# SSD slots of a two-block transformer kernel: ScalarE's queue re-ordered, C B formed ahead of the transposes and read ahead of the convolution

## The reference

```python
def ssd_mixer(h, w_in, conv_w, conv_b, dt_bias, a_log, d_skip, norm_g, w_out):
    z, xbc, dt = split(h @ w_in)
    xbc = silu(causal_depthwise_conv(xbc, conv_w, conv_b))      # 4 taps
    xs, b_in, c_in = split(xbc)
    dt = softplus(dt + dt_bias); a = -exp(a_log)
    a_cs = cumsum(dt * a)                                       # along the tokens
    decay = exp(where(causal, a_cs[l] - a_cs[s], -inf))
    cb = einsum('bclgn,bcsgn->bcgls', c_c, b_c)
    y = einsum('bcgjls,bcsgjp->bclgjp', cb * decay, x * dt) + ...
    y = y + xs * d_skip
    g = y * silu(z)
    g = g * rsqrt(mean(g * g, per group) + EPS) * norm_g
    return g @ w_out
```

## Time and profile before

| | us |
|---|---|
| median of 3 runs | 1209.87 (1209.8 to 1210.95) |
| profiled execution, its own time | 1210.28 |
| its span in the trace | 1208.6 |
| PE busy | 1148.3 (95%) |
| DVE busy | 754.4 (62%) |
| ACT busy | 674.9 (56%) |
| POOL busy | 186.3 (15%) |

### The profile page before, as it was taken

How to read it: one execution, slowest core, us unless ns; L and a number is a source line. 1 busy time by engine, 2 the same in 40 slices (tenths; PEclk the granted TensorE clock), 3 DMA queues, 4 the chain that set the end, 5 groups by cost and what they waited for, 6 DMA issues and landing times.

```text
span 1208.6 us, 23743 instructions
## 1 busy us (share of the span) xinstructions
PE 1148.3 (95%) x8898; PEld 1089.9 (90%) x8898; DVE 754.4 (62%) x1123; ACT 674.9 (56%) x1071; POOL 186.3 (15%) x134
## 2 busy tenths in 40 slices
PE   6999999999999999679988999999999999999998
PEld 5988988899999999556657999999998999999998
DVE  4788778768665554536646666555678678666543
ACT  4788888755554343457735555444554665555332
POOL 0443444317000001022301000000000212000000
PEclk8999999999999999779979999999999999999999
DMA  5554344395555554222203555565544555555553
GB/s 192 179 173 151 130 158 154 113 256 159 180 174 168 182 165 157 88 86 88 80 26 111 186 191 181 183 192 179 170 159 125 172 185 184 188 177 188 192 179 99
DMA packets 53225, 190.32 MB, mean 157 GB/s; under 512 B 5920, under 2 KB 7072, under 8 KB 53168
## 3 DMA queue, kind: packets, MB, share of 16 engines
q1 hardware_dynamic: 51408, 182.95, 47.0%
q0 software_dynamic: 1760, 6.59, 1.8%
HBM read 188.44 MB, written 1.08 MB: 157 GB/s over the span
## 4 chain that ended last, share of the span: by engine, by line
PE 75%; DVE 8%; issue 8%; ACT 5%; POOL 3%; DMA 1%; ACTq 0%; DVEq 0%; POOLq 0%; SPq 0%
PE lin L412 23%; PE lin L414 22%; PE lin L413 22%; DVE w_lo L1207 2%; POOL w_lo L1747 1%; ACT w_hi L826 1%; POOL y L1765 1%; PE lin L641 1%; PE ps L682 1%; PE ps L683 1%; PE lin L639 1%; DVE cv L1286 1%; PE ps L445 1%; DVE rot_a L1509 0%; DVE x_lo L1217 0%
## 5 line engine op out<-in xcount | busy, mean ns | idle before, releaser
L1207 DVE TENSOR_TENSOR w_lo<-w_raw,w_hi 128x1024 fp32r<-128x1024 f32 x303 | 381.3, 1260 | 273.1 <-ACT w_hi L826 273.0
L826 ACT ACTIVATE w_hi<-w_raw 128x1024 fp32r<-128x1024 f32 (+2 forms) x343 | 354.3, 1040 | 244.3 <-PE lin L414 239.9
L412 PE MATMUL lin<-x_hi,w_hi 128*128 128x256 f32 (+1 forms) x1528 | 445.4, 291 | 11.0 <-DVE x_lo L1233 3.7
L414 PE MATMUL lin<-x_hi,w_lo 128*128 128x256 f32 (+1 forms) x1528 | 439.0, 287 | 0.0
L413 PE MATMUL lin<-x_lo,w_hi 128*128 128x256 f32 (+1 forms) x1528 | 438.2, 287 | 0.0
L412 PEld LDWEIGHTS lin<-x_hi,w_hi 128*128 128x128 f32 x1528 | 292.0, 191 | 15.2 <-DVE x_lo L1233 4.1
L413 PEld LDWEIGHTS lin<-x_lo,w_hi 128*128 128x128 f32 x1528 | 291.5, 191 | 1.4 <-issue 1.0
L414 PEld LDWEIGHTS lin<-x_hi,w_lo 128*128 128x128 f32 x1528 | 292.3, 191 | 0.0
L414 PE MATMUL lin<-hid_hi,w_lo 128*128 128x256 f32 (+1 forms) x768 | 218.2, 284 | 0.0
L413 PE MATMUL lin<-hid_lo,w_hi 128*128 128x256 f32 (+1 forms) x768 | 217.9, 284 | 0.0
L412 PE MATMUL lin<-hid_hi,w_hi 128*128 128x256 f32 (+1 forms) x768 | 217.4, 283 | 0.0
(11 more groups left out here) (252 smaller groups left out, 1515.7 us busy)
## 6 DMA issues: line engine op xcount, KB each, us to landing
w_raw<-w SPq DMA_DIRECT2D x343, 512.0 KB, 3.3
acs_bc<-acs_dram POOLq DMA_DIRECT2D x8, 544.0 KB, 4.9
bias_mask<-rpb POOLq DMA_DIRECT2D x4, 512.0 KB, 9.6
h<-h SPq DMA_DIRECT2D x4, 272.0 KB, 3.7
out<-h SPq DMA_DIRECT2D x8, 128.0 KB, 3.4
cst<-const SPq DMA_DIRECT2D x1, 784.0 KB, 8.4
vecs<-vec SPq DMA_DIRECT2D x1, 131.5 KB, 2.1
acs_dram<-y POOLq DMA_DIRECT2D x1, 34.0 KB, 2.5
```

The costliest lines, as they stand in the source:

```text
L412: mm3(o, wh, xh, start=first and i == 0, stop=False)
L414: ins = mm3(o, wl, xh, start=False, stop=last and i == kts - 1)
L826: a(w_hi[pg.slot][:, 0:n], w_raw[pg.slot][:, 0:n], ACT.Copy).then_inc(w_hi_done, pages)
L1207: tt(w_lo[pg.slot][:, 0:n], w_raw[pg.slot][:, 0:n], w_hi[pg.slot][:, 0:n].bitcast(F32), ALU.subtract)\
```

## The change

ScalarE's list of a slot is written in another order: the decays and z's sigmoid come first, the two pages of chunk c+2 stand on both sides of the first taps, `decay_logs` of the first half comes before x's sigmoid and that of the second half before the sigmoid of B and C, `hi` of page (c+3, 0) comes after x's sigmoid, and `g_hi` after the last sigmoid. On PE, C B is formed before the transposes. On DVE, C B is read out of its bank before the convolution, and x's `silu` comes ahead of a page's low half. GpSimd's list and SP's are as they were.

```diff
                 if has_scan:
+                    cb_products(s + (-1))
                     x_transposes(s + (-1))
-                    cb_products(s + (-1))
...
             def slot(s, has_lin=True, has_scan=True, has_stat=True):
                 c = s.times(3, C_GRP)
                 g, gs = s + (-1), s + (-2)
-                if has_lin:
-                    hi((c + 2).page(0))
-                    hi((c + 2).page(1))
                 if has_scan:
                     decay(g, 0)
                     decay(g, 1)
+                    kz = g.times(3, K_GRP + 2)
+                    act.wait_ge(drained[kz.parity], kz.half + 1)
+                    sigmoid(z_sg[:, :, :], zg_step, g.times(3), z_raw[:, :, :])
+                if has_lin:
+                    hi((c + 2).page(0))
+                    conv0(s, 0)
+                    hi((c + 2).page(1))
                 if has_stat:
                     act.wait_ge(y2_done, (gs + 1).value)
                     a(h_sq[:, 0:2, :], y2[:, :, :], ACT.Square).then_inc(ysq_done, 1)
                 if has_lin:
-                    conv0(s, 0)
-                    hi((c + 3).page(0))
+                    if s.base:
+                        decay_logs(s, 0)
                     act.wait_ge(clamped, s.times(2, 1).value)
                     sigmoid(sg[:, 0:2, :], sg_step, s.times(6))
-                if has_scan:
-                    kz = g.times(3, K_GRP + 2)
-                    act.wait_ge(drained[kz.parity], kz.half + 1)
-                    sigmoid(z_sg[:, :, :], zg_step, g.times(3), z_raw[:, :, :])
-                if has_lin:
+                    hi((c + 3).page(0))
                     conv0(s, 1)
                     hi((c + 3).page(1))
                 if not has_lin:
                     hi2(s + (C_SOUT - 6))
-                if has_lin and s.base:
-                    decay_logs(s, 0)
...
                 if has_lin:
+                    if s.base:
+                        decay_logs(s, 1)
                     hi((c + 4).page(0))
+                    act.wait_ge(clamped, s.times(2, 2).value)
+                    sigmoid(sg[:, 2:4, :], sg_step, s.times(6, 3))
...
                 if has_lin:
-                    act.wait_ge(clamped, s.times(2, 2).value)
-                    sigmoid(sg[:, 2:4, :], sg_step, s.times(6, 3))
                     if not s.base:
                         decay_logs(s, 0)
-                    decay_logs(s, 1)
+                        decay_logs(s, 1)
                     hi((c + 4).page(1))
...
                 if has_lin:
                     lo((c + 2).page(0))
+                    if has_scan:
+                        causal_cb(g)
                     conv(s, 0)
                     clamp(sg[:, 0:2, :], cv[:, 0:2, :]).then_inc(clamped, 1)
                 if first:
                     dt_columns()
                 if has_scan:
                     scaled_tokens(g)
-                    causal_cb(g)
+                    if not has_lin:
+                        causal_cb(g)
...
                 if has_lin:
+                    silu(s, 0, xs_s[s.parity][:, :, :], cv[:, 0:2, :], sg[:, 0:2, :])
                     lo((c + 3).page(0))
-                    silu(s, 0, xs_s[s.parity][:, :, :], cv[:, 0:2, :], sg[:, 0:2, :])
```

## The result

| | before | changed |
|---|---|---|
| median | 1210.05 us (4 runs) | 1240.36 us (4 runs) |
| range | 1209.8 to 1210.95 | 1233.03 to 1243.66 |
| ratio, 95% interval | 1 | 1.0241 (1.0195 to 1.0287) |
| span in the trace | 1208.6 | 1238.5 |

The account below looks back on a forecast made before the run. PE, at 22.9 us of work per slot, was taken as the bound before, ACT at 29.03 after. Chained starts put slot 8's transposes at 255.85 instead of 224.73, +31.1 us, so 1241.0 us, range 1233 to 1252.

Parts of the forecast that it names:

- ACT's round: ACT's cycle in a full slot: 6.39 to the square, 8.70 to the logs, 13.94 from there on, 29.03 us.
- The walk: Sum of starts from slot 0's logs to slot 8's transposes, at 255.85 instead of 224.73, +31.1 us.
- The landing: POOL's DMA of `acs_bc`: data there 4.9 us behind the issue; 6 to 7.5 us a rival at 12 in 100.
- The fit of 3.3 us: Skill's price for the 544 KB DMA; by it the wait is 1.6 us shorter in seven slots, time about 1230.
- The clock: PE's slow restart at chunk c' costs 1.4 us, last slot only; low throughout: 1245 to 1251, 10 in 100.
- the 2.4 us to spare: Chunk c' ends at +16.05 with low clock, ahead of ACT's next first taps at 18.45 behind the logs.
- PE's idle time: PE idles about 5 us in each slot, most of it ahead of chunk c'.
- what the change should remove: In the SSD slots, six PE waits, 9.8 us, and two slots at low clock, 1.4 us each: about 13 us.
- the first rival: ACT's wait for the DMA costs nothing: 1197 us; turns over at a 4.2 us wait per slot; 3 in 100.

Follow-up runs that it names:

- e2: The changed kernel with POOL's DMA of the next group's cumulative sums issued one slot earlier; 1199.38 us, 0.9916 of the kernel before.
- e7: e2 with, in slot 0 alone, page (c+3, 0) ahead of x's sigmoid on ACT, its low half ahead of DVE's silu; 1197.47 us, again 1195.51.
- e4: The kernel before with only the two moves of C B, on PE and DVE, and ACT's old order; 1209.43 us, 0.9994 of the kernel before.
- e8: The kernel before with ScalarE's new list and the DMA a slot early, C B in its old places; 1200.55 us, 0.9922 of the kernel before.
- e1: The changed kernel with POOL's DMA of the cumulative sums ahead of the low half of page (c+2, 1); 1217.67 us, 1.0071 of the kernel before.
- e9: The changed kernel with the DMA issued right behind POOL's y2, first in the list in slot 1; 1200.61 us, 0.9909 of the kernel before.
- e5: The kernel before with ScalarE's new list alone, PE's and DVE's lists as before; 1245.10 us, 1.0281 of the kernel before.

## Why the prediction was right

- *ACT's round.* Foretold 29.03 us, measured 29.10 in slot 4. Up to the square 6.39 foretold and 6.39 measured (136.83 to 143.22), square to logs 8.70 and 8.79, the rest 13.94 and 13.92. The operations kept their durations in the new order, and the DMA its 4.9.
- *The walk.* Logs of slot 1: 67.25 foretold, 66.15 measured; of slot 7: 239.8 and 239.11; transposes of slot 8: 255.85 and 255.36. Some 0.6 of the 1.1 in slot 1 is that everything in this trace stands that much earlier (ACT's pages of slot 0 begin at 25.94 instead of 26.50). The rest is slot 0: the logs began at 47.72 instead of 47.87, so 0.4 later than before by that count and not 1.0, since DVE's clamp, which runs beside POOL's low half of a page there, took 2.37 us instead of 2.90.
- *The landing.* 4.8 to 5.1 in all eight, that of slot 1 among them: the row at 7.5 did not come back. That the spacing of POOL's low halves is the reason, as argued, is not shown: in e2, where the DMA goes out between low halves too, the landing took 4.0 to 6.4 us. The fit of 3.3 us that the Trainium skill gives (DMA: Bandwidth & Descriptors, section Anatomy of one DMA) is not borne out.
- *The clock.* Granted at 0.88 to 0.94 in the slots, hidden behind ACT, as the 2.4 us to spare had it, and paid in the last slot alone, as foretold: from its logs to the transposes 16.25 us (239.11 to 255.36), foretold 16.05.
- *PE's idle time* was 3.4 to 5.2 us ahead of each chunk c' from slot 1 on, instead of "about 5".

**Where a step failed.** The part on what the change should remove put six waits and two falls of the clock, 13 us, down to C B's late read, with PE as the only bound at 22.9 us. The sizes were near: the slots run at 22.6 without waits (e2), and the gain is 10 us (e2) to 13 or 16 (e7). The cause was wrong: e4 takes away just those waits and gains nothing, e8 leaves C B where it was and gains as much as e2, as far as the runs can tell. ACT's old order was a bound of 24.6 us by itself (in e4), with POOL's y2, DVE's clamp and z_s as its waits; the prediction saw that ACT had little room (21 of 24 us) but did not add its waits to its work. They stand in the trace of the kernel before, 74 to 225 us, beside the wait of PE that was read first:

```profile
DVE cv L1286 <- ACT cv L896: 16.1, 6, 3.2
...
ACT sg L881 <- DVE sg L1296: 10.0, 6, 1.8
...
ACT h_sq L933 <- POOL y L1765: 4.1, 4, 1.1
ACT g_hi L961 <- DVE z_s L1376: 3.7, 6, 0.6
```

In slots with all three waits of ACT they make some 3.5 us, so a round of 24.3 against the 25.06 measured per slot. And the first line shows, together with e8, what made C B's read late: the convolution ahead of it waited for ACT's first taps.

The turning point of the first rival, a wait of 4.2 us, was a little high: by the line from the changed kernel through e1 the time of the kernel before is reached at some 25 us of wait in all, 3.5 in each of seven slots. What makes the difference no run separates. The new order's cost in slot 0 may be part of it, but e7 leaves open what slot 0 is worth.

## What to carry to other kernels

When an operation moves forward in one engine's list, look up who fills its input, and walk that producer's list from its last release to the landing; an issue left in place on another queue can become the longest part of the way. Add up for each engine its work and its waits per round: if two rounds are within a few tenths of each other, removing one wait may gain nothing until the other is gone too. A wait is worth no more than what it does not cover: 2.1 us on the DMA in e9 cost almost nothing, since they replaced the wait for the clamp.

## What was not expected of the hardware

A clamp on DVE, from SBUF to SBUF, takes 0.44 or 0.45 us alone, and up to 3.00 where POOL is at a page's low half when it starts. In the kernel before, the clamp of x in the full slots came after the low half (in slot 4 at 132.53, POOL done at 132.20) and took 0.45; in the new order it falls beside it. In e2 this is in ACT's round, since x's sigmoid waits for the clamp; in the changed kernel the wait for the DMA hides it. Here it stands in slot 4 of the changed kernel, against POOL's row at 144.67 above, which ends at 147.07:

```profile
145.73 1.64 DVE L1296 TENSOR_SCALAR sg<-cv 128x544 f32<-128x544 f32 x1
147.29 1.07 DVE L1316 TENSOR_TENSOR x_tok<-ps,cols 128x256 f32<-128x256 f32 x3
```

The clamp ends 0.3 us behind POOL's operation. That holds in all twelve traces: of the 188 clamps of x or of B and C between 30 and 235 us, 124 begin when an operation of POOL has 0.2 us or more left, and each of these ends 0.29 to 0.32 us behind it. One clamp, in e5, begins 0.04 us ahead of POOL's low half (85.47 and 85.51): it takes 0.45 us, and this time it is POOL's operation that is longer, 2.67 us instead of some 2.4. In the slot shown the convolution just ahead of the clamp, which reads PSUM, kept its 2.51 us beside the same POOL operation. That agrees with what the Trainium skill says (SBUF — State Buffer, section Who interferes with whom): a copy-like DVE operation in a two-port mode and a GpSimd operation shut each other out for the whole instruction, one with a single SBUF input outside those modes does not. That the clamp runs in such a mode is inferred from its time; no row names the mode. No run moved POOL's page away from the clamp in the new order, so what the 1.2 us would be worth was not tried; in e2, where PE never waits, that may well be nothing. DVE's `g_lo` (L1330), which reads two operands out of SBUF, is met in the same way: 3.06 us for a pair in slot 4 of the changed kernel, beside POOL's low half, and 0.91 in the kernel before. Over the whole kernel these two kinds of operation take 19.7 us more than before, and DVE's low halves, which now stand clear of POOL more often, 9.4 less; that is where DVE's 9 us more come from.
